# Prompt attention three units ahead, reordered beginnings of three stages, and 32-row products in four column groups

## The reference

```python
shift1, scale1, gate1, shift2, scale2, gate2 = split(silu(c) @ w_ada + b_ada, 6)
h    = x * (1 + scale1) + shift1
proj = h @ w_in                       # q, k, v (512 columns each) and B, C, u (512 each)
# four heads, two attention maps of width 64 each, values of width 128
A1, A2 = softmax(q1 k1^T / 8 + bias), softmax(q2 k2^T / 8 + bias)   # bias from distance buckets, causal
oA   = rmsnorm((A1 - lam * A2) @ v) * subln_w * (1 - lam_init)
oB   = B * dwconv3_causal(C * u)
x    = layernorm(alpha * x + gate1 * (concat(oA, oB) @ w_out))
h2   = x * (1 + scale2) + shift2
# experts: 8 heads; scores against 2 x 128 keys, the best 16 x 16 pairs, 16 experts for each head
q    = (h2 @ w_pq).reshape(rows, 8, 2, 128);  s = q . sub_keys
e, g = best 16 experts of each head, softmax of their scores
f    = sum over 128 experts of  g * gelu(peer_u[e] . h2) * peer_v[e]
x    = layernorm(alpha * x + gate2 * f)
```

## Time and profile before

| | |
|---|---|
| median of 3 runs | 4086.42 us (4084.97 to 4090.69) |
| profiled execution | 4087.26 us, of which its span is 4085.4 us |
| busy share of the span | PE 60%, DVE 62%, ACT 36%, POOL 31% |
| mean granted PE clock | 0.71 of 2.4 GHz |
| DMA | 1343.86 MB, 329 GB/s over the span |

### The profile page before, as it was taken

How to read it: one execution, slowest core, us unless ns; L and a number is a source line. 1 busy time by engine, 2 the same in 40 slices (tenths; PEclk the granted TensorE clock), 3 DMA queues, 4 the chain that set the end, 5 groups by cost and what they waited for, 6 DMA issues and landing times. The chain is left out here.

```text
span 4085.4 us, 54925 instructions
## 1 busy us (share of the span) xinstructions
PE 2453.5 (60%) x16502; PEld 1093.5 (27%) x16502; DVE 2541.4 (62%) x6416; ACT 1462.2 (36%) x4211; POOL 1280.8 (31%) x1334
## 2 busy tenths in 40 slices
PE   5999756689695456464465455455446446546543
PEld 3445534466442112121121122012112112112110
DVE  1101145466474788677667767767767767866775
ACT  0110033233201456543444444444444344444443
POOL 0000000234200334444344444444434444444442
PEclk8999968899797666576576567557567557657655
DMA  9102130899724789999999999999999999999997
GB/s 352 52 22 60 27 1 1 305 410 413 281 89 162 316 364 419 403 421 420 412 419 421 416 410 417 418 413 417 417 399 421 415 411 417 421 418 415 417 420 328
DMA packets 245930, 1343.86 MB, mean 329 GB/s; under 512 B 47288, under 2 KB 60825, under 8 KB 94084
## 3 DMA queue, kind: packets, MB, share of 16 engines
q0 software_dynamic: 164352, 1174.49, 69.8%
q1 hardware_dynamic: 58704, 134.61, 9.8%
q10 hardware_dynamic: 22580, 31.27, 2.2%
HBM read 1319.30 MB, written 20.97 MB: 328 GB/s over the span
## 5 line engine op out<-in xcount | busy, mean ns | idle before, releaser
L1532 PE MATMUL psum<-sb_ring,sb_fold_weighted 128*32 128x256 f32 x8448 | 1009.6, 572 | 1300.7 <-PEq L62 1224.0
L1730 DVE CUSTOM_DVE_ANT_0 sb_ring<-sb_ring,sb_h_four 128x1024 f32<-128x1024 f32 x1056 | 1265.4, 1224 | 652.4 <-DMA sb_ring<-in_uv,sb_experts 614.5
L1500 POOL DMA_INDIRECT sb_ring<-in_uv,sb_experts x1056 | 1135.5, 1075 | 1682.8 <-POOLq L62 1525.8
L1532 PEld LDWEIGHTS psum<-sb_ring,sb_fold_weighted 128*32 128x32 f32 x8448 | 264.3, 134 | 2016.2 <-issue 2009.0
L1635 ACT ACTIVATE sb_gelu<-sb_dots 128x1 f32<-128x1 f32 x1056 | 210.4, 199 | 995.0 <-ACTq L62 988.9
L793 POOL DMA_DIRECT2D sb_v_pages<-in_cache_v x256 | 134.9, 527 | 938.8 <-issue 753.1
L1640 ACT ACTIVATE sb_fold_weighted<-sb_fold,sb_expert_w 128x32 f32<-128x32 f32 x1056 | 339.3, 321 | 34.4
L1555 PE MATMUL psum<-sb_w_pq,sb_h2T 128*128 128x512 f32 x576 | 337.4, 740 | 10.0 <-PEq L62 7.3
L1637 ACT ACTIVATE sb_expert_w<-sb_gelu,sb_gates 128x1 f32<-128x1 f32 x1056 | 311.2, 295 | 34.6
L377 PE MATMUL psum<-sb_w_qkv,sb_hT_tile 128*128 128x512 f32 (+1 forms) x432 | 189.1, 598 | 0.0
L1614 ACT COPY sb_h_four<-sb_h_tiles 32x1024 f32<-32x1024 f32 x180 | 187.5, 1042 | 4.2
(11 more groups left out here) (218 smaller groups left out, 2671.7 us busy)
## 6 DMA issues: line engine op xcount, KB each, us to landing
sb_k_pages<-in_cache_k SPq DMA_DIRECT2D x256, 256.0 KB, 6.2
sb_v_pages<-in_cache_v POOLq DMA_DIRECT2D x256, 256.0 KB, 6.3
sb_w_ada<-in_w_ada SPq DMA_DIRECT2D x12, 2048.0 KB, 17.4
sb_ring<-in_uv,sb_experts POOLq DMA_INDIRECT x1056, 13.3
sb_w_pq<-in_w_pq ACTq DMA_DIRECT2D x4, 2048.0 KB, 12.8
sb_w_qkv<-in_w_in SPq DMA_DIRECT2D x3, 2048.0 KB, 19.4
sb_w_bcu<-in_w_in SPq DMA_DIRECT2D x12, 512.0 KB, 6.3
sb_h_tiles<-h_scratch SPq DMA_DIRECT2D x9, 512.0 KB, 8.0
```

The costliest lines, as they stand in the source:

```text
L1500: pool.indirect_dma_start(ring[:, slot, :], None, uv, bass.IndirectOffsetOnAxis(ap=experts[:, u, g, n:n + 1], axis=0))\
L1532: ins = nc.tensor.matmul(psum[q * NS:(q + 1) * NS, bank, at:at + QUARTER], fw[:, slot, :], ring[:, slot, D + q * QUARTER:D + (q + 1) * QUA ...
L1730: dot = nc.vector.tensor_tensor_reduce(ring[:, slot, 0:D], ring[:, slot, 0:D], h2x[:, half], 1.0, 0.0, ALU.mult, ALU.add, dots[:, slot:slo ...
```

## The change

Five places are written in another way.

1. In `project` and in `mix` the 32 sample rows are multiplied in four column groups: 96 products of 128 columns in place of 24 of 512 in `project`, 32 of 256 in place of 16 of 512 in `mix`. ACT then copies four pieces of 32 partitions where one copy (or, in `mix`, none) stood. In `mix` these pieces go to `t1`, so ACT waits until DVE is through with the last prompt tile (`t1_free`).
2. In `prompt_attention` `scores` and `biased` run three units ahead in place of two, ACT does `exps` ahead of `turned`, and the products of one score unit alternate between the two maps (the two halves of the 128 partitions).
3. In `sample_attention` PE begins with the first key chunk; queries, bias table and `setup` follow at the steps that need them.
4. In `mix` the `ROWS` loads move from ACT to SP, behind `w_out`.
5. In `peer` all first loads but the first quarter of `w_pq` move from ACT to SP, between the first and the second tile of h2.

```diff
                         for k in range(KD):
+                            if t is None:
+                                for g in range(PILES):
+                                    cols = slice(j * AW + g * PILE, j * AW + (g + 1) * PILE)
+                                    ins = nc.tensor.matmul(psum[g * NS:(g + 1) * NS, 2 + j, 0:PILE], hTt[:, u, k, 0:n], w[:, k, cols],
+                                                           start=(k == 0), stop=(k == KD - 1), skip_group_check=True)
+                                continue
...
-                        if j < 2:
+                        if t is None:
+                            for g in range(PILES):
+                                out = qk[0:n, u, j * AW + g * PILE:j * AW + (g + 1) * PILE] if j < 2 else vo[0:n, u, g * PILE:(g + 1) * PILE]
+                                step(nc.scalar.copy(out, psum[g * NS:(g + 1) * NS, 2 + j, 0:PILE]))
+                        elif j < 2:
...
-                    for m in range(2):
-                        rows = slice(m * DH, (m + 1) * DH)
-                        for b, at in enumerate(range(0, keys, BANK)):
-                            n = min(BANK, keys - at)
+                    for b, at in enumerate(range(0, keys, BANK)):
+                        n = min(BANK, keys - at)
+                        for m in range(2):
+                            rows = slice(m * DH, (m + 1) * DH)
...
-                heads((2, scores), (1, turn), (0, values))
+                heads((3, scores), (1, turn), (0, values))
...
-                heads((1, combined), (2, biased))
+                heads((1, combined), (3, biased))
...
-                heads((1, turned), (2, exps), (0, output))
+                heads((2, exps), (1, turned), (0, output))
...
-                pe.wait_ge(T["setup"], 1)
                 turn_keys(0)
                 for k in range(STEPS + 2):
                     if k + 1 < STEPS:
                         turn_keys(k + 1)
+                    if k == 0:
+                        pe.wait_ge(T["q_ready"], 1)
                     if k < STEPS:
                         score(k)
+                    if k == 0:
+                        bias()
+                    if k == 2:
+                        pe.wait_ge(T["setup"], 1)
...
                 copy_keys(0)
+                position_rows()
                 for k in range(STEPS + 2):
                     b, c = k // NCH, k % NCH
                     if k + 1 < STEPS:
                         copy_keys(k + 1)
                     if k < STEPS:
                         maxima(k)
+                    if k == 0:
+                        bias()
...
                 sp.dma_start(w[:], A["w_out"][0].rearrange("(k p) n -> p k n", p=P)).then_inc(T["w_land"], 16)
+                for src, dst in ROWS:
+                    sp.dma_start(dst, src).then_inc(T["rows_land"], 16)
...
+                    if t is None:
+                        for k in range(KD):
+                            lhsT = oT[:, u, k, 0:n] if k < H else c_now[:, u, k - H, 0:n]
+                            for q in range(PILES):
+                                ins = nc.tensor.matmul(psum[q * NS:(q + 1) * NS, 1, 0:PILE], lhsT, w[:, k, q * PILE:(q + 1) * PILE],
+                                                       start=(k == 0), stop=(k == KD - 1), skip_group_check=True)
+                        ins.then_inc(T["pile_psum"], 1)
+                        return
...
-                for src, dst in ROWS:
-                    act.dma_start(dst, src).then_inc(T["rows_land"], 16)
...
+                    if t is None:
+
+                        take(act, T["pile_psum"])
+                        act.wait_ge(T["t1_free"], 1)
+                        for q in range(PILES):
+                            step(nc.scalar.copy(t1[0:NS, q * PILE:(q + 1) * PILE], psum[q * NS:(q + 1) * NS, 1, 0:PILE]))
+                        step.tell(T["mix_psum"])
...
                 load(0, 0)
+                sp.dma_start(sc[:], A["sub_keys"][0].rearrange("h q n d -> n (h q) d")).then_inc(T["sub_land"], 16)
+                sp.dma_start(iota[:], A["const_iota"]).then_inc(T["consts"], 16)
+                sp.dma_start(fold[:], A["const_fold"]).then_inc(T["consts"], 16)
+                for n in range(1, 4):
+                    load_w(sp, n)
                 load(1, 1)
+                for j, name in enumerate(("ln2_g", "ln2_b")):
+                    sp.dma_start(lng[:, j], A[name].to_broadcast([P, D])).then_inc(T["ln_land"], 16)
...
-                load_w(0)
-                act.dma_start(sc[:], A["sub_keys"][0].rearrange("h q n d -> n (h q) d")).then_inc(T["sub_land"], 16)
-                act.dma_start(iota[:], A["const_iota"]).then_inc(T["consts"], 16)
-                act.dma_start(fold[:], A["const_fold"]).then_inc(T["consts"], 16)
-                for n in range(1, 4):
-                    load_w(n)
-                for j, name in enumerate(("ln2_g", "ln2_b")):
-                    act.dma_start(lng[:, j], A[name].to_broadcast([P, D])).then_inc(T["ln_land"], 16)
+                load_w(act, 0)
```

79 lines of the change are left out of this document (46 added, 33 removed).

## The result

The changed kernel takes 3988.63 us (median of 4 runs, 3983.9 to 3991.51) against 4086.6 us before (median of 4 runs, 4084.97 to 4090.69): a ratio of 0.9758, with a 95% interval of 0.9741 to 0.9775. The prediction was 3995 us, with a range of 3977 to 4038.

The account below looks back on a forecast made before the run. The untouched gather loop, bound by its DMA engines, was most of the span; stages ahead had separate limits, their gains passing one for one. Terms 14 + 50 + 6 + 9.5 + 0.8 + 11 = 91.3 us less gave 3995 us, range 3977 to 4038.

Parts of the forecast that it names:

- Sample tile: In `project`: products in column groups take 5.9 us in place of 20.79, only the last block's copies show; -14 us.
- Rival C: In `project`: the column groups run one behind another, 14 us less gained, 4009 us; chance 2%.
- Prompt attention: Running three units ahead cuts DVE's 70.6 us wait ahead of the reciprocal to 13.1; -50 us after deductions.
- 6 us for PE and DVE being equally long: In prompt attention: taken off the gain because two engines that are equally long do not overlap fully.
- rival A: In prompt attention: PE becomes the bound because its clock stays at 0.50; about 4038 us, chance 11%.
- the strip wait "stays": In prompt attention: the first `biased` waits 19.69 us for the bias strip, and that wait stays.
- Sample attention: Its begin: PE turns keys some 8 us earlier, values load as before, so half the transfer shortfall is gained; -6 us.
- the 11.8 us: In sample attention's begin: the shortfall of the transfers against 408 GB/s, the most that can be gained.
- `mix`: Begin: `w_out` loads alone, PE starts 13 to 14 us after the stage's begin, -9.5 us; end about -0.8.
- `peer`: Its begin: sub keys land at 1290.5, first queries come 11.6 us earlier, 17 us after the begin; -11 us.
- Rival B: Begins of sample attention, `mix`, `peer`: another transfer lands last, -6 us in place of -27; about 4016 us, chance 8%.
- D: The gather loop loses rate, each per cent costing 27 us; a 4% loss gives about 4104 us; chance 2%.

Follow-up runs that it names:

- state_turned: Changed kernel, with PE turning the convolution's last rows so SP stores 72 rows of 512 bytes, not 9216 elements of 4 bytes: 3981.42 us, ratio to before 0.9748.
- peer_queue_only: Changed kernel, with the first quarter of `w_pq` on SP ahead of the sub keys in place of on ACT: first queries at 16.3 us, first gather at 52.8.
- strip_first: Changed kernel, with SP waiting for the four bias strips before it stores the convolution's last rows: 3993.23 us, ratio to before 0.9767.

## Why the prediction was right

**The sum.** The time lies 6 us below the forecast, 0.2% of it. By stages, in the order of the table, the errors are -0.5, -5.3, -1.7, +1.9 and +0.8 us. The four small ones add up to +0.5 by luck; prompt attention carries the rest.

**Sample tile.** -14.5 against -14, with 5.45 us for the products where 5.9 was taken from the earlier trace rows, and the warning of the Trainium skill, "TensorEngine Tiling (Array Packing)", section "Performance Considerations", did not come true here: the copies' 1.1 us a block stay below PE's 1.8. Rival C is out.

**Prompt attention.** The mechanism was right, the term mis-sized by 5.3. What was left ahead of the reciprocal (11.7) was foreseen (13.1). The step that failed is what was taken off behind that, 6 us for PE and DVE being equally long and 1 for one more `biased`: the wait ahead of `biased`, where both would show, grew by 4.5. Another 1.4 are the handover (11.7 for 13.1). PE had 40.91 us of work in the first 58, more than DVE's 37.69, and DVE still kept its pace. The clock first stood at 1.0 at 38 us from the first `biased`, before at 58, so rival A did not come. Nor is PE the bound as it is: in state_turned, with the full clock from 24 us on, PE works 101.4 us in place of 109.3, and the rest of the stage is only 2.5 us shorter. DVE works 104.9 of the 149.8 us; that it is the bound is likely and not shown. The text gave the credit mainly to the depth; the runs show that the depth and ACT's order do little without each other (3.2 and 5.5 us). That the strip wait "stays" held for the two profiles compared (18.5 and 18.6) and for no law: it varies from 12.3 to 20.8.

**Sample attention.** -7.7 (or 4 to 8, by the spread) against -6. The size fits, the reason is not shown. The step by which the products with values stand as before, and the loads of values with them, was wrong: the fourth load of values went out 2.9 us earlier. The early keys, on which the term rested, were worth nothing that can be told from the spread. That half of the 11.8 us was about right is luck as far as these runs go.

**`mix`.** -8.4 against -10.3. The step that failed is `w_out` landing 13 to 14 us after the stage's begin. That begin was read as 1097.0, the end of the stage ahead; the first load goes out at 1098.1, so 12 to 13 was meant by the same clock, and PE's first turn came at 15.4. The first gate came 7.9 us earlier, not 9.5. The transfers are slow until 1024.3 and then at 404 GB/s:

```profile
1021.00:1024.30 3.30, 0.00 (x0) 0.00 (x0) 0.00 (x0) 0.00 (x0) 2.33 (x4) 0.50 0.40 71
1024.30:1036.00 11.70, 0.00 (x0) 0.00 (x0) 2.25 (x13) 1.89 (x3) 0.00 (x0) 0.50 1.02 404
```

Two things had not been counted. The load of `subln` (L1193), one row spread over 128 partitions, stands ahead of `w_out` on SP's queue. And up to 1036 us 5.0 MB were moved, 0.7 more than `subln` and `w_out` hold, so loads from behind `w_out` had a share of the engines before PE began (up to 1.7 us at that rate). Which of the two cost more no run shows. The end of the stage gave about what was expected, 0.6 by its row against 0.8.

**`peer`.** -10.2 against -11, by a working with two errors. The stage's begin was read as 1277.3, the end of `mix`'s last issue; its first load goes out at 1280.8, so the first queries had been 25.0 us behind the begin, not 28.5. And the sub keys landed at 12.8 us, together with the quarter of `w_pq`, since the two queues share the engines; so the queries came 8.7 us earlier, not 11.6. The first gather still came 9.5 earlier. That 10.2 at the end is so near to 11 is luck, with two errors in the working and a stage that varies by 5 us. Rival B is out in `mix` and `peer`.

**Gather loop.** 387 and 415 GB/s against 392 and 414, so D did not come, and the gains stood one for one.

## What to carry to other kernels

When an engine waits in a pipeline of three engines, follow the ring and not the single wait: deeper prefetch and the order on the middle engine were worth 3.2 and 5.5 us apart and 55 together, so an experiment with either alone would have thrown the idea away. Earlier work on one engine counts only up to the next thing that lands or copies: 7 us earlier queries and one more chunk of prefetch gave nothing that stands out of the noise. And before a transfer's landing is worked out, count what stands ahead of it on its queue and what shares the engines, small loads and small packets first.

## What the runs showed of the hardware that was not expected

- 9216 stores of 4 bytes, 37 KB in all, keep the DMA engines busy for 40 to 50 us and hold up larger loads beside them: the first `biased`, which waits for the four bias strips (2.3 MB), came 9.6 to 10.5 us after the stage's begin without them and 12.3 to 20.8 us with them.
- Two queues that load at once share the engines: the 2 MB quarter of `w_pq` is there 9.1 us after the first load when the 1 MB of sub keys follows it in one queue, and 12.6 to 13.9 beside it.
- Stops of PE, ACT and DVE at once, of 5.5 and 8.1 us, came in prompt attention while 4-byte packets were moved (in peer_queue_only, whose rest is 8 us longer, and in strip_first), but not in the other runs with these packets, and not in state_turned. Their cause is open.
- Loads of instructions (8 and 16 KB) took up to 8.2 us while the 4-byte packets were moved, and at most 1.4 us in all of state_turned.
